# Row norm and layer norm ahead of the third layer, from sums over the same pieces

## The reference, cut to what matters

```python
EPS, EPS_2 = 1e-6, 1e-5

def rmsnorm(x, w):                       # end of first_block
    y = x * lax.rsqrt(jnp.mean(x * x, axis=-1, keepdims=True) + EPS)
    return y * w

def first_block(...):
    for i in range(DEPTH):
        ...
        x = x + gate * y                 # y: output product of the layer
    return rmsnorm(x, final_norm_w)      # first norm; its result is the residual stream of block two

def second_block(x, ln_mix_g, w_in, b_in, ...):
    h = x
    xn = rmsnorm_2(h, ln_mix_g[l])       # second norm, same form, EPS_2
    z = xn @ w_in[l] + b_in[l]           # 1024 x 3840 input product
    ...
    h = h + merged @ w_o[l]
    h = h + peer(rmsnorm_2(h, ln_ffn_g[l]), ...)
    return rmsnorm_2(h, ln_final_g)
```

## Time and profile before

| what | us |
|---|---|
| median of 3 runs | 1782.33 |
| the profiled execution, whole | 1781.56 |
| its span | 1779.8 |
| TensorE busy in the span | 1684.2 (95%) |
| VectorE busy | 1164.0 (65%) |
| ScalarE busy | 923.0 (52%) |
| GpSimd busy | 352.6 (20%) |

### The profile page before, as it was taken

How to read it: one execution, slowest core, us unless ns; L and a number is a source line. 1 busy time by engine, 2 the same in 40 slices (tenths; PEclk the granted TensorE clock), 3 DMA queues, 4 the chain that set the end, 5 groups by cost and what they waited for, 6 DMA issues and landing times.

```text
span 1779.8 us, 34361 instructions
## 1 busy us (share of the span) xinstructions
PE 1684.2 (95%) x11772; PEld 1554.7 (87%) x11772; DVE 1164.0 (65%) x2348; ACT 923.0 (52%) x1688; POOL 352.6 (20%) x223
## 2 busy tenths in 40 slices
PE   6899989999999997899999999989999999999998
PEld 5899778888889876898899999989999988888887
DVE  2686367777544655438755999977888765555554
ACT  1665523232344553545443544458988855545544
POOL 2000000000000000310001777766656500000000
PEclk9999999999999998899999999999999999999999
DMA  9655310101735332442563565554445455565653
GB/s 277 196 177 184 118 49 24 47 24 48 245 111 163 118 110 72 147 143 81 172 146 92 168 170 165 167 153 141 143 131 143 143 187 191 192 197 189 193 195 131
DMA packets 211808, 255.54 MB, mean 144 GB/s; under 512 B 15911, under 2 KB 193803, under 8 KB 211723
## 3 DMA queue, kind: packets, MB, share of 16 engines
q1 hardware_dynamic: 211723, 254.39, 47.1%
HBM read 253.29 MB, written 1.05 MB: 143 GB/s over the span
## 4 chain that ended last, share of the span: by engine, by line
PE 74%; DVE 10%; DMA 5%; issue 4%; ACT 4%; SPq 2%; DVEq 0%; POOL 0%; ACTq 0%; POOLq 0%
PE ps L1902 20%; PE ps L2409 20%; PE ps L2391 9%; DMA raw<-in_u_experts 4%; PE ps L2379 3%; PE ps L1922 2%; PE ps L2052 2%; PE ps L2041 2%; DVE raw L1677 2%; PE ps L2053 2%; PE ps L2132 2%; SPq L529 2%; PE ps L2031 2%; PE ps L1973 1%; PE ps L2199 1%
## 5 line engine op out<-in xcount | busy, mean ns | idle before, releaser
L643 POOL TENSOR_TENSOR w_lo<-raw,w_hi 128x1024 fp32r<-128x1024 f32 x128 | 307.6, 2406 | 342.2 <-ACT w_hi L1056 342.2
L1902 PE MATMUL ps<-x_hi,w_hi 128*128 128x256 f32 x1088 | 313.8, 288 | 12.1 <-DVE x_lo L1188 7.0
L1902 PE MATMUL ps<-x_lo,w_hi 128*128 128x256 f32 x1088 | 309.4, 284 | 0.0
L1902 PE MATMUL ps<-x_hi,w_lo 128*128 128x256 f32 x1088 | 309.3, 284 | 0.0
L1863 DVE TENSOR_TENSOR w_lo<-raw,w_hi 128x1024 fp32r<-128x1024 f32 x124 | 152.0, 1226 | 143.3 <-ACT w_hi L1156 143.3
L1902 PEld LDWEIGHTS ps<-x_hi,w_hi 128*128 128x128 f32 x1088 | 210.4, 193 | 16.1 <-issue 9.8
L1156 ACT ACTIVATE w_hi<-raw 128x1024 fp32r<-128x1024 f32 x124 | 131.6, 1061 | 168.0 <-PE ps L2409 168.0
L1902 PEld LDWEIGHTS ps<-x_lo,w_hi 128*128 128x128 f32 x1088 | 210.5, 193 | 0.3 <-issue 0.2
L1902 PEld LDWEIGHTS ps<-x_hi,w_lo 128*128 128x128 f32 x1088 | 210.2, 193 | 0.0
L1056 ACT ACTIVATE w_hi<-raw 128x1024 fp32r<-128x1024 f32 x128 | 134.8, 1053 | 120.9 <-DVE raw L1677 120.8
L2354 PE MATMUL ps<-x_hi,w_hi 128*128 128x256 f32 x576 | 166.7, 289 | 10.2 <-ACT arena L1078 10.2
(11 more groups left out here) (366 smaller groups left out, 3918.6 us busy)
## 6 DMA issues: line engine op xcount, KB each, us to landing
raw<-in_u_experts SPq DMA_DIRECT2D x512, 128.0 KB, 2.7
raw<-in_v_experts SPq DMA_DIRECT2D x128, 512.0 KB, 4.3
arena<-in_ada_w SPq DMA_DIRECT2D x20, 1024.0 KB, 5.2
raw<-in_a_w_in SPq DMA_DIRECT2D x12, 1024.0 KB, 5.3
arena<-in_a_w_in SPq DMA_DIRECT2D x12, 1024.0 KB, 5.4
raw<-in_b_w_in SPq DMA_DIRECT2D x8, 1024.0 KB, 5.6
arena<-in_b_w_in SPq DMA_DIRECT2D x8, 1024.0 KB, 5.7
raw<-in_w_in SPq DMA_DIRECT2D x8, 1024.0 KB, 5.4
```

What stands on the lines that cost most here:

```text
L643: pool.tensor_tensor(UTL[e], UT[e % 2], UTH[e].bitcast(F32), ALU.subtract).then_inc(utl_ready, 1)
L1902: ins = mm(o[:, b * S:b * S + S], w[:, slot, kk, b * P:b * P + P], xx[:, (kk + turn) % KC, :], start=(kk == 0 and n == 0), stop=(kk == k - ...
```

## The change: what it does

The two norms are made from sums taken of the pieces of X as they are finished, in the form that the norm ahead of the expert layer has already.

With Y = X * w (w the weight of the first norm), the two norms in a row are, before the second weight, Y times one factor per token: rsqrt(mean(Y^2) + 1e-5 * (mean(X^2) + 1e-6)). So:

- VectorE writes Y (at the place of H) piece by piece behind each `residual`, by an added 128 x 512 multiply with FNW.
- ScalarE squares each piece of X and of Y with row sums (`squares_two`): four passes of 128 x 256 a piece.
- VectorE makes the bias YB of the logarithm: from the first three pieces of Y ahead of the last `residual`, and with the sum over X behind the last piece.
- One logarithm for each token group and one exponential give the factor. VectorE scales Y into XN in four parts of 128 x 512.
- TensorE's transposes wait for half of them at block 0 and at block 4. XHI and XLO are written block by block from PSUM with the second weight, H is gone, and `x_halves` waits for two blocks at a time (`wo_lo`) in this product also.
- The factor of the first norm alone (RSTD1) is made by ScalarE behind the eight blocks, and X = Y * RSTD1 by VectorE behind the low half of the second T_CIN tile.
- `x_ready` goes to 4 in one step, behind the last multiply for Y.

The diff, cut to its core (what is left out shifts counts of semaphores in later stages by what is added here):

```diff
+        SSY = MC[:, 8:16].rearrange("p (t u) -> p t u", t=TT)
+        YB = MC2
+        JUNKY = at(T0 + 6144, 2048).rearrange("p (a n) -> p a n", a=TT)
+        RSTD1 = MC[:, 2:4]
+        Y = at(T0 + 2048, 2048).rearrange("p (a n) -> p a n", a=TT)
+
+        def bo_block(k):
+            return ps[2 + k // 2][:, (k % 2) * S:(k % 2) * S + S]
 # ScalarE
-            for u in range(4):
-                hi(T_BOUT, 0, u + 1)
-            statistics(2, eps6)
-            norm(3, lambda k: COLS[:, CMX + k:CMX + k + 1], None, eps5, 52, 5)
+            def squares_two(u):
+                cols = slice(TW * u, TW * u + TW)
+                act.wait_ge(res_m, 5 + u)
+                for t in range(TT):
+                    act.activation(JUNK[:, t, cols], X[:, t, cols], ACT.Square, accum_out=SSP[:, t, u:u + 1]).then_inc(nt_ss, 1)
+                act.wait_ge(nt_xn, 4 + u + 1)
+                for t in range(TT):
+                    act.activation(JUNKY[:, t, cols], Y[:, t, cols], ACT.Square, accum_out=SSY[:, t, u:u + 1]).then_inc(nt_ss, 1)
+
+            hi(T_BOUT, 0, 1)
+            for u in range(3):
+                hi(T_BOUT, 0, u + 2)
+                squares_two(u)
+            squares_two(3)
+            act.wait_ge(nt_ss, 4 + 16)
+            act.wait_ge(fin_bias, 4)
+            for t in range(TT):
+                act.activation(lnss[:, t:t + 1], SSY[:, t, 3:4], ACT.Ln, scale=1.0 / D, bias=YB[:, t:t + 1]).then_inc(nt_ln, 1)
+            act.wait_ge(nt_ln, 2 + 2)
+            act.activation(rstd, lnss, ACT.Exp, scale=-0.5).then_inc(nt_rstd, 1)
+            act.wait_ge(tile_done, 52 + 2)
+            for k in range(KC):
+                if k % 2 == 0:
+                    act.wait_ge(nt_T, 8 + k // 2 + 1)
+                act.activation(XHI[:, k, :], bo_block(k), ACT.Copy, scale=COLS[:, CMX + k:CMX + k + 1]).then_inc(nt_h, 1)
+            act.sem_inc(xhi_ready, 2)
+            act.activation(MC[:, 0:2], ss, ACT.Ln, scale=1.0 / D, bias=eps6).then_inc(nt_ln, 1)
+            act.wait_ge(nt_ln, 2 + 3)
+            act.activation(RSTD1, MC[:, 0:2], ACT.Exp, scale=-0.5).then_inc(nt_rstd, 1)
 # VectorE
             for u in range(4):
                 lo(T_BOUT, 0, u + 1)
+                if u == 3:
+                    v.wait_ge(nt_ss, 4 + 12)
+                    v.tensor_reduce(YB, SSY[:, :, 0:3], AX_X, ALU.add).then_inc(fin_bias, 1)
+                    v.wait_ge(fin_bias, 1)
+                    v.tensor_scalar(YB, YB, 1.0 / D, 1e-5 * 1e-6, ALU.mult, ALU.add).then_inc(fin_bias, 1)
                 residual(T_BOUT, u, 1)
-            v.wait_ge(res_m, 8)
-            v.sem_inc(x_ready, 1)
-            v.wait_ge(fn_in, 16)
-            row_norm(2, FNW)
-            v.wait_ge(nt_row, 2)
-            v.sem_inc(x_ready, 1)
-            norm(3)
-            split_x(5, H)
-            lo(T_CIN, 0, 1)
+                if u == 0:
+                    v.wait_ge(fn_in, 16)
+                cols = slice(TW * u, TW * u + TW)
+                v.wait_ge(res_m, 5 + u)
+                v.tensor_tensor(Y[:, :, cols], X[:, :, cols], bcast(FNW[:, cols], 2), ALU.mult).then_inc(nt_xn, 1)
+            v.sem_inc(x_ready, 2)
+            v.wait_ge(nt_ss, 4 + 14)
+            v.tensor_reduce(ss, SSP, AX_X, ALU.add).then_inc(fin_bias, 1)
+            v.wait_ge(fin_bias, 3)
+            v.scalar_tensor_tensor(YB, ss, 1e-5 / D, YB, ALU.mult, ALU.add).then_inc(fin_bias, 1)
+            v.wait_ge(nt_xn, 4 + 4)
+            v.wait_ge(nt_rstd, 2 + 1)
+            for half in range(2):
+                for t in range(TT):
+                    cols = slice(512 * half, 512 * half + 512)
+                    v.tensor_scalar(XN[:, t, cols], Y[:, t, cols], rstd[:, t:t + 1], None, ALU.mult).then_inc(nt_xn, 1)
+            for k in range(KC):
+                if k % 2 == 0:
+                    v.wait_ge(nt_h, 16 + k + 2)
+                v.scalar_tensor_tensor(XLO[:, k, :], bo_block(k), COLS[:, CMX + k:CMX + k + 1], XHI[:, k, :].bitcast(F32),
+                                       ALU.mult, ALU.subtract).then_inc(wo_lo, 1)
+            v.sem_inc(x_split, 2)
+            lo(T_CIN, 0, 1)
+            v.wait_ge(nt_rstd, 2 + 2)
+            for t in range(TT):
+                v.tensor_scalar(X[:, t, :], Y[:, t, :], RSTD1[:, t:t + 1], None, ALU.mult).then_inc(nt_row, 1)
+            v.wait_ge(nt_row, 2)
 # TensorE
-                if x_round[0] == 9:
+                if x_round[0] in (5, 9):
                     if kk % 2 == 0:
-                        pe.wait_ge(wo_lo, kk + 2)
+                        pe.wait_ge(wo_lo, 2 * (x_round[0] - 5) + kk + 2)
...
-            norm(3)
+            for k in range(KC):
+                if k % 4 == 0:
+                    pe.wait_ge(nt_xn, 8 + k // 2 + 2)
+                for t in range(TT):
+                    ins = pe.transpose(bo_block(k)[:, t * P:t * P + P], XN[:, t, k * P:k * P + P], ident)
+                if k % 2:
+                    ins.then_inc(nt_T, 1)
             x_round[0] = 5
```

More of the change, by code:

```diff
@@ L1037, in _ @@
             squares(3)
-            act.wait_ge(nt_ss, 8 + 8)
-            act.wait_ge(fin_bias, 2)
+            act.wait_ge(nt_ss, 20 + 8)
+            act.wait_ge(fin_bias, 4 + 2)
             for t in range(TT):
                 act.activation(lnss[:, t:t + 1], SSP[:, t, 3:4], ACT.Ln, scale=1.0 / D, bias=SSB[:, t:t + 1]).then_inc(nt_ln, 1)
-            act.wait_ge(nt_ln, 4 + 2)
+            act.wait_ge(nt_ln, 5 + 2)
             act.activation(rstd, lnss, ACT.Exp, scale=-0.5).then_inc(nt_rstd, 1)
@@ L1164, in _ @@
                                    accum_out=SQP[:, t, h:h + 1]).then_inc(nt_ss, 1)
-                act.wait_ge(nt_ss, 16 + 2 * t + 2)
-                act.wait_ge(fin_bias, 2 + t + 1)
+                act.wait_ge(nt_ss, 28 + 2 * t + 2)
+                act.wait_ge(fin_bias, 6 + t + 1)
                 act.activation(lnss[:, t:t + 1], SQP[:, t, 1:2], ACT.Ln, scale=1.0 / D, bias=SQB[:, t:t + 1]).then_inc(nt_ln, 1)
-                act.wait_ge(nt_ln, 6 + t + 1)
+                act.wait_ge(nt_ln, 7 + t + 1)
                 act.activation(rstd[:, t:t + 1], lnss[:, t:t + 1], ACT.Exp, scale=-0.5).then_inc(nt_rstd, 1)
@@ L1651, in _ @@
                 if u == 3:
-                    v.wait_ge(nt_ss, 8 + 6)
+                    v.wait_ge(nt_ss, 20 + 6)
                     v.tensor_reduce(SSB, SSP[:, :, 0:3], AX_X, ALU.add).then_inc(fin_bias, 1)
-                    v.wait_ge(fin_bias, 1)
+                    v.wait_ge(fin_bias, 5)
                     v.tensor_scalar(SSB, SSB, 1.0 / D, 1e-5, ALU.mult, ALU.add).then_inc(fin_bias, 1)
@@ L1868, in _ @@
             for t in range(TT):
-                v.wait_ge(nt_ss, 16 + 2 * t + 1)
+                v.wait_ge(nt_ss, 28 + 2 * t + 1)
                 v.tensor_scalar(SQB[:, t:t + 1], SQP[:, t, 0:1], 1.0 / D, 1e-5, ALU.mult, ALU.add).then_inc(fin_bias, 1)
@@ L2321, in _ @@
                 if k % 4 == 0:
-                    pe.wait_ge(nt_xn, 6 + k // 2 + 2)
+                    pe.wait_ge(nt_xn, 12 + k // 2 + 2)
                 for t in range(TT):
```

## The result

The changed kernel takes 1773.1 us, the median of four runs (1771.17 to 1775.18), against 1782.63 for four runs of the kernel before: a ratio of 0.9943, 95% interval 0.993 to 0.9955. That is 9.5 us; forecast were 9.4 and 1772.9. The execution whose profile follows took 1774.77 us with a span of 1773.0, so it lies above the median, and by the profiles alone the gain is 6.8 us.

What follows compares the result with a forecast made beforehand. TensorE, busy 95% of the span, bounds the kernel, so gain lies only where it stands still around the two norms. First T_CIN tile done at 719.13 instead of 728.55: 1782.33 - 9.4 = 1772.9 us; range 1770.7 to 1776.0.

Steps and rivals of the forecast that it cites:

- Steps 1 to 5: From T_BOUT's end to the first transpose: squares, logarithms and scalings replace the old norms; start 709.17 instead of 715.52.
- E: Some wait still ties the factor to work behind the last piece; gain only about 2.5 us, 1779.8; chance 0.03.
- Step 6: Transposes into the first T_CIN product: no TensorE pause at low clock, first product at 712.84, 8.0 us earlier.
- Step 7: TensorE's clock low after the 5.0 us pause, back at 713.6; 0.8 us of the first T_CIN tile low, costing 0.36.
- B: Clock comes back late because transposes count for little; 18 matmuls low, gain 8.0 us, 1774.3; chance 0.19.
- A: Clock stays full through the 5.0 us pause, transposes take 1.91; gain 10.7 us, 1771.6; chance 0.09.
- D: Slower: low clock holds on through the T_CIN tiles; held for three tiles, 1786.6; chance 0.02.
- The covers: Slack before TensorE waits: 0.6 us for the second T_CIN tile's low half, 1.3 us under the T_BOUT tiles.
- The early loads: Pooling load and GpSimd's small row start at about 706.4 instead of 711.18, with nothing near waiting for them.
- C: Part given back: second T_CIN tile's low half late, or T_BOUT tiles stretch; gain 6.5 us, 1775.8; chance 0.07.

Runs made afterwards that it cites:

- the kernel with the sums only: Changed kernel keeping its sums, but with the old half-width H, XHI and XLO path behind the transposes; 1776.09 us, ratio 0.9958 to before.
- the Y multiply four times: Changed kernel with VectorE's Y multiply done four times for the first three pieces, result not used; 1773.37 us, one run.
- the blocks only: Kernel before with its statistics and row norm kept, but XHI and XLO written in blocks from PSUM; 1777.85 us, ratio 0.9983.
- the fill: Changed kernel with 40 unused matmuls in the pause between the last T_BOUT tile and the transposes; 1770.67 us, in another set 1770.77.

## Why the prediction was right, by its own steps

Steps 1 to 5, the chain up to the first transpose, are right: forecast +4.95, measured +4.99. Squares 1.72 (forecast 1.75), logarithms to VectorE's start 0.85 (0.84), two scalings up to TensorE's start 0.94 (0.89). The bias was ready at about 707.8, ahead of the logarithm at 708.21, as taken, and the Y multiply took 0.69. No wait for a row norm or a second statistics is left in the chain, so E is out.

Step 6, no pause behind the transposes: right, shown by the timeline after and, in reverse, by the kernel with the sums only. The first product came at +8.31 instead of +8.62, 0.3 early: the 3.67 of the earlier trace rows includes the last transpose's run to its end, and the next matmul starts beside it.

Step 7, the clock, is right in kind (low behind this pause, back during the unbroken work) and is the term that was mis-sized. The low clock lasted 5.9 us from the first transpose (709.98 to 715.9) where I had taken 4.4. Of the first tile 2.6 us ran low, 12 matmuls at 0.22, which cost 1.2 instead of 0.36. With the 0.3 from step 6 that leaves the stretch 0.57 longer than forecast: 15.48 for 14.91. The sign that the clock would be at 1.00 within a microsecond of the first product failed in this profile; in the second one it held (1.0 us).

It is not a constant: measured from the first transpose the clock was back after 3.0, 4.3, 5.6, 5.7, 5.9 and 6.1 us in six profiles of the changed kernel and its variants with the same unbroken work. The forecast says 4.4 and B 7.2, so the runs lie on both sides of the forecast, four of them about half-way to B, and its margin of 0.3 for the clock was too small. What differs is when the clock fell: 2.5 to 4.3 us behind the end of T_BOUT in five of the six, each then low for 6.8 us. In the sixth, with the Y multiply four times, it fell 5.1 us behind and was low for 3.4. Why it falls sooner in one execution than in another stays open.

B's mechanism, that transposes count for little, is not borne out: with the blocks only, and with the sums only, the clock came back 2.9 us after the first transpose, before any product. A needed the fill. D did not occur in any profile: the clock was at 1.00 by 6.1 us after the first transpose in each profile without a second pause.

The Trainium skill ("TensorE: Matmul & The Clock Gate", section "What's actually happening") says that the low state is the default and that activity lifts it. The traces agree: 0.50 behind the pause of 5.0 us, 1.00 again during the work behind it, and 1.00 through the whole stretch where the pause was filled. That unbroken transposes count as such activity is not in that section; the prediction drew it from there, and it is the two profiles with the return at 2.9 us that show it.

The covers: 1.4 us for the second tile's low half in the profile after (forecast 0.6), and 0.4 in the filled kernel; about 1.3 for the T_BOUT tiles, as worked out, and these still follow each other at 5.76; the scaling of X hidden at 718.99, with the next low half not before 723. The early loads changed nothing that can be seen. From the end of the first T_CIN tile to the pause ahead of the attention it took the same 75.7 us, so nothing of C was given back there.

That the median came within 0.2 of the forecast is partly luck. For the profiled execution the same forecast was 1772.2, and it took 1774.77: 0.6 is the longer stretch, 0.8 the later start and 1.3 the attention. The stretch gained 8.8 to 9.6 against one profile of before, while medians of four to six runs of one kernel, or of two with the same stretch, differ by up to 3 us between sets.

## What to carry to other kernels

Where a dense engine waits for a chain over two others, take the sums during the last products, so that only the last piece's share stands in the wait, and look for two norms in a row that reduce to one factor. Hand the split input over in blocks of the size in which it is consumed; a copy of half the width at a time costs a pause of its own, and at the low clock a part of it does not show (1.66 us there, 2.79 at the full clock). Read a step's worth from the distance between landmarks on both sides of it, since single runs here vary by as much as the step is worth.

## What the runs showed of the hardware that was not expected

Useless matmuls in a pause give back what the low clock cost only as far as the path behind them can follow: in the stretch of the kernel before 1.2 us of 3.5, in the changed kernel 1.7 us of the 2.9 of its first profile (1.0 to 1.8 over three profiles). Neither shows clearly in the time. The clock falls at the attention's pause of 2.18 us in eight of the fourteen profiles and not in the others, and stays low for different times with the same work behind; the attention behind such a pause took 56.9, 58.4 and 59.7 us with the clock low for none, 3.4 and 6.8 us of it. Executions of one kernel on one chip lie up to 9 us apart. The varying clock explains a few of these. In the second profile of the filled kernel T_BOUT ended at 707.0 and not at 703.5. The traces show where the 3.5 come from: behind pauses of 1.83 and 2.20 us (which end at 483.6 and 564.8) the clock fell for 3.4 us each time, which the other profile does not have, and each cost about 1.5 us; it was already 1.3 late at 480 us, and 0.7 is taken off again by a fall near 677 that only the other profile has.
